# The head of a hybrid backbone: tokens turned, shifted and scaled by pairs of feature chunks while the modulation weights arrive

## Chip, cores and metric

One core of a Trainium2 chip runs the whole kernel. The metric is the device time of one execution in microseconds (us). The engines are TensorE (PE: matmuls, and PEld: its weight loads), VectorE (DVE), ScalarE (ACT), GpSimd (POOL), and SyncE (SP), which issues most of the loads.

## What is computed

Four layers (SSD mixer, attention, pooling mixer, SSD mixer) with one residual stream of 512 tokens (256 of context, 256 latent) and 1024 features. The head works for the first layer alone:

```python
shift, scale, gate = split(silu(c) @ mod_w + mod_b)   # once for the latent tokens' c, once for c_ctx
h = x * (1 + scale) + shift                           # 512 tokens x 1024 features
zxbcdt = h @ w_in                                     # first layer: 1024 -> z, x, B, C, dt
dt = softplus(dt + dt_bias)                           # a chain of small elementwise steps
xbc = silu(depthwise_conv(xbc))                       # five taps
```

## The kernel before

**Exact products.** Every large product is made of three passes. An operand is split into a part rounded for the matmul (`w_hi`, `h_hi`) and the rest (`w_lo`, `h_lo`); `three_pass` (L436 on) multiplies hi by hi, hi by lo and lo by hi into one PSUM bank. ACT makes the hi part (L397 for weights, `act_split`), DVE the lo part (L406, `dve_split`), each behind a load into one of the four slots of `raw`.

**Order.** Each engine runs its own list in the order of the code; counting semaphores tie the lists together. SP issues the loads in the order of `items`: a unit of weights is 1024 columns for 128 partitions, and slot r waits until the unit that lay in it four items earlier is split or summed.

**The head.** The first layer's shift and scale are eight pieces (`HEAD_MODS`) of 256 of the 2048 outputs: pieces 0 to 3 are the shift, 4 to 7 the scale. Each piece comes by two loads of 512 KB to places that are free at that time (`ys`, `xc`, `y`, `xw`, `cb`, `Wa`, `Wb`, `Hs`). For each piece PE makes a sum (`pe_mod_sum`, L466, 16 matmuls with `c_col` as weights), ACT copies the sum out of PSUM (`act_mod_rows`, L486), PE turns it into columns (`pe_mod_turn`, L491), and DVE adds the bias (`dve_mod_col`, L498). The turn of a piece stands behind the sum of the next. The semaphore of a load covers two pieces (`head_full[q // 2]`).

When all eight are in, `dve_ab` (L1688) makes scale and shift columns `ab`; the tokens, turned by PE into features x tokens 128 tokens at a time (`pe_turn`, L1617), are scaled tile by tile, by ACT for tiles 0 and 2 (`act_affine`, L1628, hi part L1634) and by DVE for tiles 1 and 3 (L1667, lo part L1679). `pe_begin` then projects dt and the first x for the first 256 tokens, `ssd_pe_dt` and `ssd_project` with k of 0 and 1 for the other 256. `pe_dt_turn` (L1221) turns the dt rows, and `ssd_dve_start` computes dt from them (L1314 on), with the splits of the first B/C weights (`bc`) and of the second x in between. `taps` (L929) is the convolution; its coefficients `gp` are 24 small copies (L1306, L1308).

Of the kernel before, what the change touches and what calls it, by code (L numbers as in the profile page):

```python
# [3 lines left out]
def backbone(nc, ins, out, depth=4):  # L4
# [4 lines left out]
    F32, F32R = mybir.dt.float32, mybir.dt.float32r  # L9
# [5 lines left out]
    NT = 4  # L15
# [425 lines left out]
    def project(pe, o, key, t, done, t0=0, t1=TOK):  # L441


        for k in range(KT):
# [5 lines left out]
            if done is not None and ((t == 1 and k == KT // 2 - 1) or k == KT - 1):  # L450
                last.then_inc(done, 1)

    def mod_at(L, q):
        return MOD_PIECES * L + q

    def pe_mod_sum(pe, L, q, b):
        for a in range(2):
            if L == 0 and q < HEAD_MODS:
                pe.wait_ge(head_full[q // 2], 64)
                w = head_place(2 * q + a)  # L460
# [195 lines left out]
    def ssd_pe_step(pe, L, i):  # L656
# [4 lines left out]
        if i < GRP:  # L661
            ssd_project(pe, L, i, 0)
# [4 lines left out]
            ssd_project(pe, L, i, 1)  # L667
            if i >= 2:
# [621 lines left out]

    def ssd_dve_start(dve, L):
        s = lay[L]
        j = L // 3
        op, need = dt_steps(dve, s, 0)
        v, e, w, zero = (t256(Wa, k) for k in range(4))
        lnw, r, dtA, dt = (t256(Wb, k) for k in range(4))
        b4 = lambda ap: ap.unsqueeze(1).broadcast_to((128, NT, 2 * HEADS))
        q4 = lambda ap: ap.rearrange("p (c n) -> p c n", c=NT)

        for tap in range(6):  # L1300
# [8 lines left out]
        op("gp", last)  # L1309
        if L:  # L1310
            dve_resid(dve, L - 1, (2, 3))
# [13 lines left out]
        need("zero")  # L1325
        dve_split2(dve, L, "bc", 0)
        dve.wait_ge(s["dt_a"], 4)
# [185 lines left out]
    def pe_tiles_ready(pe, L, n):  # L1513

        s = lay[L - 1] if L else head
        pe.wait_ge(s["hhi_a"], s["base"]["hhi_a"] + n)
        pe.wait_ge(s["hlo_d"], s["base"]["hlo_d"] + n)
# [131 lines left out]

    def act_head_tiles(act):  # L1650

        for n in range(NT):
            if n % 2:
                act.wait_ge(hf_d, n + 1)
            else:
                act_affine(act, head, n, n, n)
            act_h_hi(act, head, n, n)

    def dve_head_tiles(dve):
        for n in (1, 3):  # L1660
            for half in range(2):
                dve.wait_ge(head["turn_p"], 2 * n + half + 1)
                if n == 3:
                    dve.wait_ge(head["hlo_d"], 2)
                for k in range(4):
                    kk = 4 * half + k
                    last = dve.tensor_scalar(hfs[1][:, kk, :], bank[2 * n + half][:, 128 * k:128 * k + 128],  # L1667
                                             ab[:, 0, n // 2, kk:kk + 1], ab[:, 1, n // 2, kk:kk + 1],
                                             ALU.mult, ALU.add)
                last.then_inc(hf_d, 1)  # L1670
            if n == 1:
                dve_split(dve, 0, "x", 0, 1)
            dve_h_lo(dve, head, n - 1, n - 1)
            dve_h_lo(dve, head, n, n)

# [806 lines left out]
    def _(sp):  # L2482
        def load_head(q):
            for a in range(2):
                d = head_place(2 * q + a).rearrange("p (k n) -> p k n", n=256)
                sp.dma_start(d, w_in_view(ins["mod_w"][0], 256 * q, 256, 4 * a, 4 * a + 4)).then_inc(head_full[q // 2], 16)  # L2486
# [55 lines left out]
    def _(act):  # L2542
# [13 lines left out]
        for t in range(NT):  # L2556
# [71 lines left out]
    def _(pe):  # L2628
# [3 lines left out]
        pe.wait_ge(par_done, 2)  # L2632
        for q in range(HEAD_MODS + 1):
            if q < HEAD_MODS:
                pe_mod_sum(pe, 0, q, 6 + q % 2)
            if q:
                if q > 2:
                    pe.wait_ge(mod_done, q - 2)
                pe_mod_turn(pe, 0, q - 1, 4 + (q - 1) % 2)
            if q == 3:  # L2640
                pe.wait_ge(par_loaded, 16 * 10)
                for t in range(1, 5):
                    n = 112 if t == 1 else 128
                    pe.transpose(bank[0][:, 128 * t - 128:128 * t - 128 + n], rows[0:n, t, :],
                                 ident[0:n, 0:n]).then_inc(par_turned, 1)
            if q == 5:
                pe.wait_ge(in_loaded, 64)
                pe_turn(pe, head, 0, 0, (par_done, 6))
                pe_turn(pe, head, 1, 1, (par_done, 6))
        pe_turn(pe, head, 2, 2, (mod_done, HEAD_MODS))  # L2650
        pe_turn(pe, head, 3, 3, (mod_done, HEAD_MODS))
        pe_begin(pe, 0, 0)
        pe_begin(pe, 0, 1)
        for L in range(depth):
            s = lay[L]
            pe_tiles_ready(pe, L, NT)
            if L % 3 == 0:
                ssd_pe_dt(pe, L, SEG, TOK)
                for i in range(GRP + 1):
# [49 lines left out]
```

## Time and profile before

| | us |
|---|---|
| median of 3 runs | 1536.99 (1532.41 to 1537.48) |
| the profiled execution, its own time | 1531.61 |
| its span | 1530.3 |
| PE, DVE, ACT busy | 1455.0, 1132.9, 705.9 |
| last load of head modulation landed | 37.7 |
| first projection begins | 49.6 |
| DVE's dt work begins | 67.1 |
| first convolution tap | 78.4 |

A row of a timeline gives the start, the time from the first start to the last end of its instructions, the engine, the line, what is written and read, and how many instructions are merged. In square brackets stands how long the engine was idle before it, and what ended that. Matmuls overlap, so the pitch between starts tells more than a duration. The span is the time between first and last instruction; the execution's own time also holds what lies around it.

### The profile page before, as it was taken

How to read it: one execution, taken by the hardware profiler on the slowest of the kernel's cores; microseconds unless marked ns; L12 is line 12 of the kernel's file. 1: busy time of each engine (PE TensorE's matmuls, PEld its weight loads, DVE VectorE, ACT ScalarE, POOL GpSimd, SP SyncE). 2: the span in 40 equal slices, each digit the busy share in tenths (PEclk: the TensorE clock that was granted, in tenths of full speed). 3: DMA queues.
4: the chain of work that ended last, by engine and by line, in shares of the span. 5: the costliest groups of instructions: out<-in, count | busy, mean ns of one | idle time of the engine just before them, and what ended most of it. 6: DMA issues, size and time to landing. Idle time of an engine off the chain costs nothing.

```text
span 1530.3 us, 22697 instructions
## 1 busy us (share of the span) xinstructions
PE 1455.0 (95%) x8557; PEld 1205.2 (79%) x8557; DVE 1132.9 (74%) x1694; ACT 705.9 (46%) x1259; POOL 329.0 (21%) x379
## 2 busy tenths in 40 slices
PE   5899999999999999999899999999999999999987
PEld 3787888888877889886678887787888889888865
DVE  0688999999996385867658555646438999999996
ACT  1554554545454253455545322323324565555552
POOL 1042344344451012001000000000001234434340
PEclk9999999999999999999999999999999999999999
DMA  9245535564453413315332436444341444434443
GB/s 325 78 139 168 149 111 167 153 192 133 121 161 130 129 45 87 122 33 174 115 120 88 137 116 195 137 130 165 100 127 29 116 111 129 120 111 115 130 130 122
DMA packets 169421, 197.38 MB, mean 129 GB/s; under 512 B 9696, under 2 KB 151648, under 8 KB 169312
## 3 DMA queue, kind: packets, MB, share of 16 engines
q1 hardware_dynamic: 158480, 163.08, 34.5%
q0 software_dynamic: 9296, 30.19, 7.5%
q10 hardware_dynamic: 1536, 2.67, 0.5%
q8 instruction: 68, 1.11, 0.3%
q14 instruction: 41, 0.34, 0.1%
HBM read 194.59 MB, written 1.31 MB: 128 GB/s over the span
## 4 chain that ended last, share of the span: by engine, by line
PE 45%; DVE 36%; issue 8%; ACT 7%; DMA 2%; SPq 2%; POOL 1%; DVEq 0%; ACTq 0%; POOLq 0%
PE ps L437 12%; PE ps L438 11%; PE ps L439 11%; DVE xc L929 7%; DVE w_lo L406 5%; DVE cum_b L937 4%; ACT w_hi L397 2%; ACT Wb L792 2%; PE ps L466 2%; DVE Wb L956 2%; SPq L2486 1%; DVE Hs L974 1%; PE ps L618 1%; PE ps L1938 1%; PE ps L624 1%
## 5 line engine op out<-in xcount | busy, mean ns | idle before, releaser
L437 PE MATMUL ps<-h_hi,w_hi 128*128 128x512 f32 (+2 forms) x1088 | 412.2, 379 | 9.6 <-issue 4.9
L439 PE MATMUL ps<-h_hi,w_lo 128*128 128x512 f32 (+2 forms) x1088 | 398.6, 366 | 0.0
L438 PE MATMUL ps<-h_lo,w_hi 128*128 128x512 f32 (+2 forms) x1088 | 398.5, 366 | 0.0
L406 DVE TENSOR_TENSOR w_lo<-raw,w_hi 128x1024 fp32r<-128x1024 f32 (+1 forms) x203 | 244.4, 1236 | 112.0 <-ACT w_hi L397 110.3
L397 ACT ACTIVATE w_hi<-raw 128x1024 fp32r<-128x1024 f32 (+1 forms) x203 | 206.5, 1050 | 134.0 <-PE ps L439 114.1
L437 PEld LDWEIGHTS ps<-h_hi,w_hi 128*128 128x128 f32 (+1 forms) x1088 | 205.8, 189 | 54.3 <-issue 19.1
L439 PEld LDWEIGHTS ps<-h_hi,w_lo 128*128 128x128 f32 (+1 forms) x1088 | 205.3, 189 | 33.8
L438 PEld LDWEIGHTS ps<-h_lo,w_hi 128*128 128x128 f32 (+1 forms) x1088 | 205.9, 189 | 30.8
L929 DVE SCALAR_TENSOR_TENSOR xc<-ps,gp,xc 128x508 f32<-128x508 f32 (+1 forms) x224 | 162.7, 727 | 17.9 <-ACT xc L761 12.0
L439 PE MATMUL ps<-w_hi,ylo 128*128 128x512 f32 x376 | 147.1, 391 | 0.0
L1136 POOL DMA_DIRECT2D cum_b<-cum_scratch x96 | 71.8, 754 | 248.0 <-PE ps L618 168.9
L437 PE MATMUL ps<-w_hi,h_hi 128*128 128x512 f32 (+1 forms) x336 | 119.1, 354 | 4.6 <-issue 2.3
L438 PE MATMUL ps<-w_lo,h_hi 128*128 128x512 f32 (+1 forms) x336 | 116.2, 346 | 0.0
L1808 POOL TENSOR_TENSOR small<-small 128x1 f32<-128x1 f32 x14 | 10.4, 741 | 463.5 <-DVE small L1742 463.5
L1155 POOL TENSOR_TENSOR xw<-xT,sg 128x256 f32<-128x256 f32 x96 | 78.9, 852 | 82.0 <-ACT xT L783 82.0
L439 PEld LDWEIGHTS ps<-w_hi,ylo 128*128 128x128 f32 x376 | 71.0, 189 | 15.1
L792 ACT ACTIVATE Wb<-cb,sg 128x128 f32<-128x128 f32 x192 | 58.8, 389 | 44.1 <-DVE cb L947 44.1
L437 PEld LDWEIGHTS ps<-w_hi,h_hi 128*128 128x128 f32 x336 | 64.2, 191 | 14.5 <-issue 3.4
L937 DVE TENSOR_TENSOR cum_b<-cum_b,sg 128x1024 f32<-128x1024 f32 x48 | 72.7, 1515 | 1.2 <-DMA cum_b<-cum_scratch 1.2
L1165 POOL TENSOR_TENSOR Wa<-cb,sg 128x512 f32<-128x512 f32 x48 | 59.1, 1251 | 56.6 <-DVE Wb L956 37.6
L438 PEld LDWEIGHTS ps<-w_lo,h_hi 128*128 128x128 f32 x336 | 64.1, 191 | 7.2
L498 DVE TENSOR_TENSOR mod_col<-ps,par 128x4 f32<-128x4 f32 x48 | 7.6, 157 | 82.5 <-PE ps L491 82.3
(265 smaller groups left out, 2611.4 us busy)
## 6 DMA issues: line engine op xcount, KB each, us to landing
raw<-in_mod_w SPq DMA_DIRECT2D x80, 512.0 KB, 4.6
raw<-in_ssm_w_in SPq DMA_DIRECT2D x64, 512.0 KB, 4.9
cum_b<-cum_scratch POOLq DMA_DIRECT2D x96, 256.0 KB, 5.6
raw<-in_ssm_w_in SPq DMA_DIRECT2D x66, 256.0 KB, 4.6
raw<-in_ssm_w_out SPq DMA_DIRECT2D x32, 512.0 KB, 4.7
raw<-in_pool_w_in SPq DMA_DIRECT2D x32, 512.0 KB, 4.8
raw<-in_attn_w_in SPq DMA_DIRECT2D x20, 512.0 KB, 4.1
raw<-in_pool_w_out SPq DMA_DIRECT2D x16, 512.0 KB, 4.7
```

Of the source, the lines that this page charges most:

```text
L397: act.activation(hi, w_shaped(key, raw[:, r % RS, :], width), ACT.Copy).then_inc(hi_done, 1)
L406: dve.tensor_tensor(lo, w_shaped(key, raw[:, r % RS, :], width), hi.bitcast(F32), ALU.subtract).then_inc(lo_done, 1)
L437: pe.matmul(o, hi_s, hi_m, start=first, stop=False)
L438: pe.matmul(o, hi_s, lo_m, start=False, stop=False)
L439: return pe.matmul(o, lo_s, hi_m, start=False, stop=last)
L466: last = pe.matmul(bank[b][32 * j:32 * j + 32, 0:256], c_col[:, 4 * a + j, :], w[:, 256 * j:256 * j + 256], start=a == 0, stop=a == 1)
L792: last = act.activation(Wb[:, n % 2, h, :], cb[:, 1, c, :], ACT.Copy, scale=sg[:, g, 48 + 4 * c + h:49 + 4 * c + h])
L929: T["tap_d"].inc(dve.scalar_tensor_tensor(ov, iv, gp[:, i, 6 * k + tap:6 * k + tap + 1], ov, ALU.mult, ALU.add))
L937: T["seg_d"].inc(dve.tensor_tensor(e, e, by_head(sg[:, g, 8 * c:8 * c + 8], (128, 8, 128)), ALU.subtract))
L1136: pool.dma_start(cum_b[:, c, d, :, :], src).then_inc(s["cum_loaded"][c], 16)
L1155: last = pool.tensor_tensor(xw[:, k, d, :].rearrange("p (h q) -> p h q", q=PH), xT[:, cs[d], :].rearrange("p (h q) -> p h q", q=PH), sprea ...
L1165: pool.tensor_tensor(Wa[:, n % 2, :, :], cb[:, 0, c, :].unsqueeze(1).broadcast_to((128, HG, 128)), spread(sg[:, g, 32 + 4 * c:36 + 4 * c], ...
```

## The change

Pieces are taken in pairs: piece n of the shift and piece n of the scale (`HEAD_ORDER` is 0, 4, 1, 5, 2, 6, 3, 7). A pair gives shift and scale for two chunks of 128 features, over all 512 tokens. PE turns a chunk (`pe_head_turn`), ACT scales the even chunk and makes both hi parts (`act_head_chunks`), DVE scales the odd one and makes both lo parts (`dve_head_affine`, `dve_head_lo`), and PE adds the chunk's share to dt and the first x, 9 matmuls over 512 columns (`pe_head_project`), before the next pair's sums. The places for the loads and the slots of `raw` are as before; the loads of dt and the first x come behind the first pair, that of the second half of x behind the second pair. The gp copies and the split of the first half of the first `bc` move into the head.

```diff
-        for q in range(HEAD_MODS + 1):
-            if q < HEAD_MODS:
-                pe_mod_sum(pe, 0, q, 6 + q % 2)
-            if q:
-                if q > 2:
-                    pe.wait_ge(mod_done, q - 2)
-                pe_mod_turn(pe, 0, q - 1, 4 + (q - 1) % 2)
...
-        pe_turn(pe, head, 2, 2, (mod_done, HEAD_MODS))
-        pe_turn(pe, head, 3, 3, (mod_done, HEAD_MODS))
-        pe_begin(pe, 0, 0)
-        pe_begin(pe, 0, 1)
+        for n in range(HEAD_MODS + 1):
+            if n < HEAD_MODS:
+                if n >= 2:
+                    pe.wait_ge(mod_done, n - 1)
+                pe_mod_sum(pe, 0, HEAD_ORDER[n], 6 + n % 2)
+            if n:
+                pe_mod_turn(pe, 0, HEAD_ORDER[n - 1], 6 + (n - 1) % 2, 256)
+            if n == 1:
+                pe.wait_ge(in_loaded, 64)
+                for k in range(3):
+                    pe_head_turn(pe, k)
...
+            if n in (3, 5, 7):
+                if n == 3:
+
+                    pe.wait_ge(par_done, 6)
+                for k in (n - 3, n - 2):
+                    pe_head_project(pe, k)
+                for k in {3: (3, 4), 5: (5, 6), 7: (7,)}[n]:
+                    pe_head_turn(pe, k)
+        for k in (KT - 2, KT - 1):
+            pe_head_project(pe, k)
```

ACT's and DVE's lists, and the new functions that they call:

```diff
+        for n, q in enumerate(HEAD_ORDER):
+            act_mod_rows(act, 0, q, 6 + n % 2)
+            if n == 1:
+                act_split(act, 0, "dt", 0, 0, width=KT * 64)
+                act_split(act, 0, "x", 0, 0)
...
+            if n % 2:
+                act_head_chunks(act, n // 2)
+            if n == 3:
+                act_split(act, 0, "x", 0, 1)
+        act_split(act, 0, "bc", 0, 0)
...
+        for n, q in enumerate(HEAD_ORDER):
+            dve_mod_col(dve, 0, q, 6 + n % 2, 256)
+            if n % 2:
+                dve_head_ab(dve, n // 2)
+                dve_head_affine(dve, n // 2)
+                if n == 1:
+                    dve_split(dve, 0, "dt", 0, 0, width=KT * 64)
+                    dve_split(dve, 0, "x", 0, 0)
+                dve_head_lo(dve, n // 2)
+            if n == 3:
+                dve_split(dve, 0, "x", 0, 1)
+            if n == 5:
+                dve.wait_ge(par_done, 6)
+                ssd_dve_taps_par(dve, 0)
+        dve_split(dve, 0, "bc", 0, 0)
...
+    def act_head_chunks(act, n):
+
+        k = 2 * n
+        act.wait_ge(head["ab_d"], n + 1)
+        act.wait_ge(head["turn_p"], k + 1)
+        if n >= 2:
+            act.wait_ge(head["hlo_d"], k - 3)
+        for st in range(2):
+            c = slice(SEG * st, SEG * st + SEG)
+            last = act.activation(head_hf(k)[:, c], head_bank(k)[:, c], ACT.Identity, scale=ab[:, 0, st, k:k + 1],
+                                  bias=mod_col[:, 0, k, st:st + 1])
+        last.then_inc(head["hf_a"], 1)
+        act.wait_ge(head["hf_a"], n + 1)
+        act.activation(h_hi[:, k, :], head_hf(k), ACT.Copy).then_inc(head["hhi_a"], 1)
+        act.wait_ge(hf_d, n + 1)
+        act.activation(h_hi[:, k + 1, :], head_hf(k + 1), ACT.Copy).then_inc(head["hhi_a"], 1)
...
+    def pe_head_project(pe, k):
+
+        s = lay[0]
+        pe.wait_ge(head["hhi_a"], k + 1)
+        pe.wait_ge(head["hlo_d"], k + 1)
```

And SP's, where a load's place in the list is its turn:

```diff
-        for q in range(HEAD_MODS - 2):
-            load_head(q)
+        for n in range(2):
+            load_head(n)
         for r, (kind, n, key) in enumerate(items):
-            if r == 2:
-                for q in range(HEAD_MODS - 2, HEAD_MODS):
-                    load_head(q)
+
+            if r in (2, 3):
+                for n in range(2, 4) if r == 2 else range(4, HEAD_MODS):
+                    load_head(n)
```

**How the order moves.** On PE before, from the fifth sum to the first projection (`xc`, `y`, `xw`, `cb` and so on are places of the loaded pieces, `pick` turns a sum, `resid` are the tokens):

```order
L466 MATMUL ps<-xc,c_col 32x256 x8
L491 MATMUL ps<-pick,mod_rows 128x2 x2
L466 MATMUL ps<-y,c_col 32x256 x4
L466 MATMUL ps<-xw,c_col 32x256 x4
L491 MATMUL ps<-pick,mod_rows 128x2 x2
L1617 MATMUL ps<-ident,resid 128x128 x16
...
L491 MATMUL ps<-pick,mod_rows 128x2 x4
L1617 MATMUL ps<-ident,resid 128x128 x16
L437 MATMUL ps<-h_hi,w_hi 64x256
```

On PE in the changed kernel, the same pieces, from the last matmul of chunk 1 on:

```order
L1698 MATMUL ps<-h_hi,w_lo 128x512
L1679 MATMUL ps<-ident,resid 128x128 x8
L470 MATMUL ps<-xc,c_col 32x256 x8
L495 MATMUL ps<-pick,mod_rows 128x2 x2
L470 MATMUL ps<-y,c_col 32x256 x4
L470 MATMUL ps<-xw,c_col 32x256 x4
L495 MATMUL ps<-pick,mod_rows 128x2 x2
L437 MATMUL ps<-h_hi,w_hi 64x512
```

The first L495 row completes a pair; the second belongs to the next pair, and it stands between that completion and the projection of chunks 2 and 3.

On ACT in the changed kernel, the second pair, from the copy of its second sum (the copies of sums are L490, the chunks L1713 to L1719, the split L397):

```order
L490 ACTIVATE mod_rows<-ps 128x256
L1713 ACTIVATE hf<-ps,mod_col,ab 128x256 x2
L1717 ACTIVATE h_hi<-hf 128x512
L1719 ACTIVATE h_hi<-hf 128x512
L397 ACTIVATE w_hi<-raw 128x1024
L490 ACTIVATE mod_rows<-ps 128x256 x2
```

The copy of the next pair's first sum, for which PE's second L495 row waits, stands behind the chunks and the split. Before, no copy of a sum had a token operation ahead of it: the copies of sums were done when the first L1628 came.

## Rows read from the trace of the kernel before

**Rows 1.** The page's chain that ended last, shares by engine

```profile
PE 45%; DVE 36%; issue 8%; ACT 7%; DMA 2%; SPq 2%; POOL 1%; DVEq 0%; ACTq 0%; POOLq 0%
```

**Rows 2.** The chain in order of time, 0 to 130 us: start, us, what

```profile
28.00 9.74 DMA Hs<-in_mod_w
...
43.13 2.91 ACT hf L1628 x8
...
66.66 0.41 PE ps L1221 x4
67.09 0.44 DVE Wa L1314
...
76.04 2.35 DVE w_lo L406 x2
78.39 0.67 DVE xc L929
```

**Rows 3.** Timeline of PE, 0 to 125 us

```profile
21.65 1.94 PE L466 MATMUL ps<-ys,c_col 128*32 128x256 f32 x16 [4.67 <-DMA ys<-in_mod_w]
...
26.32 1.01 PE L491 MATMUL ps<-pick,mod_rows 128*128 128x2 f32 x4
...
33.75 3.65 PE L1617 MATMUL ps<-ident,resid 128*128 128x128 f32 x16
...
38.59 0.60 PE L466 MATMUL ps<-Wa,c_col 128*32 128x256 f32 x8
...
41.90 0.58 PE L491 MATMUL ps<-pick,mod_rows 128*128 128x2 f32 x4 [0.62 <-DVE mod_col L498]
42.73 1.97 PE L1617 MATMUL ps<-ident,resid 128*128 128x128 f32 x16 [0.26 <-DVE mod_col L498]
49.62 0.45 PE L437 MATMUL ps<-h_hi,w_hi 128*64 128x256 f32 x1 [4.92 <-issue]
...
54.55 0.41 PE L439 MATMUL ps<-h_hi,w_lo 128*64 128x256 f32 x1
...
70.73 0.50 PE L437 MATMUL ps<-h_hi,w_hi 128*128 128x512 f32 x1 [0.60 <-DVE w_lo L406]
...
76.08 0.39 PE L439 MATMUL ps<-h_hi,w_lo 128*128 128x512 f32 x1
```

**Rows 4.** Busy time by stretch: PE, PEld, DVE, ACT, POOL, granted clock, DMA, GB/s

```profile
core 0: us, PE busy (x) PEld busy (x) DVE busy (x) ACT busy (x) POOL busy (x), PEclk, DMA share, GB/s
...
28.00:32.00 4.00, 4.00 (x34) 2.06 (x36) 0.16 (x1) 1.15 (x5) 1.78 (x3) 1.00 1.10 334
...
50.00:52.00 2.00, 2.00 (x12) 2.00 (x11) 2.00 (x8) 1.97 (x5) 0.00 (x0) 0.50 0.09 29
```

**Rows 5.** Timeline of ACT, 0 to 125 us

```profile
24.63 0.38 ACT L486 ACTIVATE mod_rows<-ps 128x256 f32<-128x256 f32 x1 [7.16 <-PE ps L491]
...
34.26 1.56 ACT L397 ACTIVATE w_hi<-raw 128x512 fp32r<-128x512 f32 x2
...
41.65 1.05 ACT L397 ACTIVATE w_hi<-raw 128x1024 fp32r<-128x1024 f32 x1
...
63.83 0.59 ACT L1253 ACTIVATE y<-ps 64x512 f32<-64x512 f32 x1 [10.41 <-PE ps L439]
...
71.96 1.43 ACT L761 ACTIVATE xc<-ps,gp 128x512 f32<-128x512 f32 x2
```

**Rows 6.** Timeline of DVE, 0 to 125 us

```profile
42.51 0.16 DVE L498 TENSOR_TENSOR mod_col<-ps,par 128x4 f32<-128x4 f32 x1 [0.76 <-PE ps L491]
...
43.13 2.64 DVE L1667 TENSOR_SCALAR hf<-ps,ab 128x128 f32<-128x128 f32 x8
45.70 1.21 DVE L406 TENSOR_TENSOR w_lo<-raw,w_hi 128x1024 fp32r<-128x1024 f32 x1
...
56.45 0.17 DVE L1308 COPY gp<-par 128x8 f32<-128x8 f32 x1
...
115.59 0.68 DVE L970 COPY Hs<-ps 128x512 f32<-128x512 f32 x1
```

More of the change, by code:

```diff
@@ L451, in project @@
                 last.then_inc(done, 1)
+    HEAD_ORDER = [q for n in range(HEAD_MODS // 2) for q in (n, HEAD_MODS // 2 + n)]
     def mod_at(L, q):
-        return MOD_PIECES * L + q
+        return MOD_PIECES * L + (HEAD_ORDER.index(q) if L == 0 and q < HEAD_MODS else q)
     def pe_mod_sum(pe, L, q, b):
@@ L1294, in ssd_dve_start @@
         op, need = dt_steps(dve, s, 0)
[L1295 to L1298, printed above, removed]
         for tap in range(6):
@@ L1309, in ssd_dve_start @@
         op("gp", last)
+    def ssd_dve_start(dve, L):
+        s = lay[L]
+        if L:
+            ssd_dve_taps_par(dve, L)
+        op, need = dt_steps(dve, s, 1)
+        v, e, w, zero = (t256(Wa, k) for k in range(4))
+        lnw, r, dtA, dt = (t256(Wb, k) for k in range(4))
+        b4 = lambda ap: ap.unsqueeze(1).broadcast_to((128, NT, 2 * HEADS))
+        q4 = lambda ap: ap.rearrange("p (c n) -> p c n", c=NT)
         if L:
@@ L1325, in ssd_dve_start @@
         need("zero")
-        dve_split2(dve, L, "bc", 0)
+        for a in range(2) if L else (1,):
+            dve_split(dve, L, "bc", 0, a)
         dve.wait_ge(s["dt_a"], 4)
@@ L1648, in dve_affine_half, with head_bank @@
         last.then_inc(s["hf_a"], 1)
[L1650 to L1674, printed above, removed]
+    def head_bank(k):
+        return bank[(2, 4, 5)[k % 3]]
@@ new lines, in head_hf, with pe_head_turn @@
+    def head_hf(k):
+        return hfs[k // 2 % 2][:, :, :].rearrange("p k n -> p (k n)")[:, 512 * (k % 2):512 * (k % 2) + 512]
+    def pe_head_turn(pe, k):
+        if k >= 3:
+            pe.wait_ge(*((hf_d, (k - 3) // 2 + 1) if k % 2 == 0 else (head["hf_a"], (k - 3) // 2 + 1)))
+        for tt in range(NT):
+            last = pe.transpose(head_bank(k)[:, 128 * tt:128 * tt + 128], resid[:, tt, 128 * k:128 * k + 128],
+                                ident[:, :])
+        last.then_inc(head["turn_p"], 1)
@@ new lines, in pe_head_project @@
+    def pe_head_project(pe, k):
+        s = lay[0]
+        pe.wait_ge(head["hhi_a"], k + 1)
+        pe.wait_ge(head["hlo_d"], k + 1)
+        hi, lo = pe_unit(pe, 0, "dt", 0, 0)
+        c = slice(64 * k, 64 * k + 64)
+        last = three_pass(pe, bank[3][0:64, :], hi[:, c], lo[:, c], h_hi[:, k, :], h_lo[:, k, :], k == 0, k == KT - 1)
+        if k == KT - 1:
+            last.then_inc(s["dt_p"], 1)
+        hi, lo = pe_unit(pe, 0, "x", 0, k // 4)
+        for t in range(2):
+            c = slice(256 * (k % 4) + 128 * t, 256 * (k % 4) + 128 * t + 128)
+            pe.matmul(bank[t], hi[:, c], h_hi[:, k, :], start=k == 0, stop=False)
+            mid = pe.matmul(bank[t], hi[:, c], h_lo[:, k, :], start=False, stop=False)
+            last = pe.matmul(bank[t], lo[:, c], h_hi[:, k, :], start=False, stop=k == KT - 1)
+            if k == KT - 1:
+                if t == 1:
+                    mid.then_inc(s["x_p"], 1)
+                last.then_inc(s["x_p"], 1)
@@ new lines, in dve_head_ab, with dve_head_affine @@
+    def dve_head_ab(dve, n):
+        k = 2 * n
+        dve.wait_ge(mod_done, k + 2)
+        dve.tensor_scalar(ab[:, 0, :, k:k + 2].rearrange("p s k -> p k s"), mod_col[:, 0, KT + k:KT + k + 2, :],
+                          1.0, None, ALU.add).then_inc(head["ab_d"], 1)
+    def dve_head_affine(dve, n):
+        k = 2 * n + 1
+        dve.wait_ge(head["ab_d"], n + 1)
+        dve.wait_ge(head["turn_p"], k + 1)
+        if n >= 2:
+            dve.wait_ge(head["hhi_a"], k - 3)
+        for st in range(2):
+            c = slice(SEG * st, SEG * st + SEG)
+            last = dve.tensor_scalar(head_hf(k)[:, c], head_bank(k)[:, c], ab[:, 0, st, k:k + 1],
+                                     mod_col[:, 0, k, st:st + 1], ALU.mult, ALU.add)
+        last.then_inc(hf_d, 1)
@@ L1676, in dve_h_lo, with dve_head_lo @@
+    def dve_head_lo(dve, n):
+        dve.wait_ge(hf_d, n + 1)
+        for k in (2 * n, 2 * n + 1):
+            dve.wait_ge(head["hhi_a"], k + 1)
+            dve.tensor_tensor(h_lo[:, k, :], head_hf(k), h_hi[:, k, :].bitcast(F32),
+                              ALU.subtract).then_inc(head["hlo_d"], 1)
     def dve_h_lo(dve, s, n, tt):
```

68 lines of the change are left out of this document (27 added, 41 removed).

## The prediction

> **What bounds the kernel now.** I read the page's chain first: PE and DVE hold 45% and 36% of it, DMA 2% [rows 1]. The kernel is no load-bound kernel as a whole, but its first 50 us are another stage. So the chain in order of time comes next, for the head alone [rows 2]: it stands on the last of the eight pieces of modulation weights until 37.7 us (28.00 + 9.74), then on turns, shift and scale, and the scaling of the tokens (8 ACT operations from 43.13), and only at 49.62 does the first projection begin [rows 3]. The four dt transposes at 66.66 release DVE's dt work at 67.09; that runs to the weight splits at 76.04 and to the first convolution tap at 78.39 [rows 2]. From there DVE is named again and again, so the number that decides is not when PE finishes x, but **when DVE can start its dt work: 67.1 us today** (call it V).
>
> The head's projections are slow at first: PE had waited 4.92 us, and the 24 dt matmuls of 256 columns from 49.62 to 54.55 have a pitch of (54.55 - 49.62)/23 = 0.214 us, with the granted clock at 0.50 in 50 to 52 [rows 3, 4], i.e. 1.2 GHz. At the full clock a 512-column matmul has a pitch of (76.08 - 70.73)/23 = 0.233, less one late start; I take 0.228. Before 38 us the page's clock says 1.00, but sixteen equal transposes took 3.65 us at 33.75 and 1.97 us at 42.73 [rows 3]: I read the early stretch as slow too, rising about 38.4, between the 3.65 us of transposes and the sum at 38.59.
>
> **The change, part by part.** The total of the loads stays; one x piece (0.52 MB) moves ahead of the last four pieces of modulation. At 334 GB/s [rows 4] the last load comes 1.6 us later, 39.3.
>
> A round is now, in PE's order: sum of a piece, turn of the one before, sum, turn, project two chunks (18 matmuls of 512 columns), transpose further chunks. The turn that completes a pair stands ahead of the projection of the same pair, and the next pair's sums stand behind it. So a pair's whole chain through ACT and DVE lies open on PE. I price it from a turn's start T:
> - turn to DVE's column 0.61 (41.90 to 42.51), the column 0.16 and a scale like it, 0.4 with their starts [rows 3, 6].
> - two ACT affines of 256 columns out of PSUM: 128 columns cost 2.91/8 = 0.36, 512 cost 1.43/2 = 0.72, so 0.48 each, 1.0 together [rows 2, 5]. DVE's pair beside it: 0.33 at 128, 0.68 at 512 [rows 6], so 0.45 each, hidden.
> - two ACT copies of 512: 1.56 less the 1.05 of 1024 columns gives 0.5 to 0.6 each [rows 5]; DVE's h_lo of 512: half of 1.21, 0.65 [rows 6].
>
> The even chunk can be projected at T + 3.4, the odd one at T + 4.0. But PE first waits for the next piece's turn, and that waits for ACT's copy of the sum (0.38), which stands behind ACT's chunks: T + 4.0 in the third pair, and in the second, where the second x piece's split (1.05) stands there too, T + 5.0 [rows 5].
>
> *First pair.* Its second turn stands behind the sum of the third piece, so it waits for the second pair of loads: before, that sum began at 21.65, released by the load [rows 3]; dt and x (0.79 MB) now go ahead of it, + 2.35 = 24.0. Sum 1.9 (21.65), turn at 25.9, 1.0 at the slow clock (26.32): DVE's column at 27.0. ACT's chunks are done at 29.65, its copy of the next sum at 30.0, PE's turn at 31.0. DVE has two splits (1.8) ahead of its h_lo: ready at 30.9. **The first projection starts at 31.0.** Its price: 18 x 0.228 = 4.1 at full clock, 18 x 0.427 = 7.7 at half clock (twice the 0.214 of 256 columns). The rate rose 4.8 us after the dense work from 33.75 began, and from 49.62 it had not risen by 54.55 [rows 3]. I take 5.4 us: 12.6 slow matmuls and 5.4 fast ones, 6.6 us; ends 37.6.
>
> *Later rounds*, full clock: eight transposes 1.0 (half of 1.97), a sum 0.95 (8 matmuls 0.60 with the tail of the last, so under twice that, 38.59). Second pair's T = 37.6 + 1.95 = 39.55; projection T + 5.0 to T + 9.1; transposes and sum 1.95: third pair's T = 50.6. Projection T + 4.0 to T + 8.1, four transposes 0.5: last T = 59.2. Last projection T + 3.4 to T + 7.5 = 66.7. All loads are in at 39.3, so most of this lies after them: **only the first pair is really projected during the loads**. The dt rows are complete at 65.4, ACT's copy of them (0.6) hides, PE's transposes start at 66.7, and V = 67.2 against 67.1.
>
> *What V does not show.* 144 matmuls of 256 columns become 72 of 512: the same columns. The 24 small copies to gp move into DVE's wait for the last turn, 59.2 + 0.6 by the schedule, and cost nothing; bare they would be at most 24 x 0.17 = 4.1 us [rows 6]. The first bc split leaves the dt chain: such a pair costs 2.35 at 76.04, so 1.2 us on DVE [rows 2]; but ACT reads the dt rows at 65.4 rather than 63.8 [rows 5], so its table load, exponent and bc copy end 0.5 later, and its Exp and Ln with them. I keep 0.6 of the 1.2. PE can project bc's first half at once and then waits for the second, no longer the bound. Sum at the first tap: + 0.1 - 0.6 = **- 0.5 us**. Against the profiled execution's 1531.6 that is 1531.1; that execution lies 5.4 us below the median of the runs shown (1536.99), so the same change on the median gives 1536.5.
>
> Unknown costs, both ends. The slow stretch of the first pair: 4.1 (none slow) to 7.7 (all slow), - 2.5 to + 1.1. The three open chains, 5.0 + 4.0 + 3.4: a quarter less or more is 3.1 either way, since nothing in the trace shows 256-column affines. The clock in the later pairs: below.
>
> The notes bear on this too. Profile first: behind the sixteen transposes of 33.75 the next sums ran at the fast rate, and the transposes of 42.73 themselves took half the time [rows 3]. The Trainium skill (TensorE: Matmul & The Clock Gate, "Part 4: PE-mode transpose") says that the full clock does not engage for transposes. By that rule the transposes between my rounds would not help to hold the clock; here the trace does not agree, and the sum stays as it is.
>
> **Rivals.**
> *The clock falls between the rounds (slower).* Place: PE's wait between the second sum and the blocking turn. In the trace it fell after PE had gone idle at 44.7, and stood at half in 50 to 52 [rows 3, 4]; the complete waits of my schedule are 2.5, 1.5 and 2.9 us, shorter, but little work stands around them, only sums and turns. A pair that runs slow costs 18 x 0.2 = 3.6 us. One such pair gives + 3.1, not measurable; from two on it decides: + 6.7, 1543.7; all three with their sums and transposes about + 12, 1549. For it: the early sums up to 32 us ran slow for long. Against it: from 38.6 to 44.7 sums and turns kept the rate up. 0.16.
> *The rounds are shorter than I price (faster).* No slow stretch in the first pair and a third off the open chains: - 2.5 - 4.1 - 0.5 = - 7, 1530. For it: ACT's and DVE's chain after the loads today, on four times as many instructions, runs without gaps [rows 2]. 0.16.
> *The loads bound every round.* Then only the last pair lies behind 39.3: two sums, two turns 3.3, chain 2.8, projection 4.1, V = 50, - 17 us, 1520. It needs all three earlier projections done by 39; by the sum only one is. 0.03.
> *The change does nothing for what follows:* x is ready sooner, and the dt chain or the POOL loads behind it swallow the 0.5. 1537.0. 0.10.
> The forecast itself: 0.55.
>
> **How the numbers follow.** About 0.3% (4.6 us) is what a measurement of this kernel can tell from no change. Same: 0.55 + 0.10 = 0.65. Faster: 0.16 + 0.03 = 0.19. Slower: 0.16. The likeliest case's own range is - 4 to + 4 around 1536.5. To leave out no more than 2 in 10, the range goes from the second rival's 1530 (with a little, 1529) to 1542, which leaves out most of the slow-clock case and the load-bound one.
>
> **What would show it.** In the profile of the changed kernel: the first projection at 31, three waits of PE of 2 to 3 us each ahead of a turn of mod_rows or of a projection, named by ACT's mod_rows or h_lo; the last x matmul near 66.7; DVE's dt work at 67.2; a tap at 77.9. Each pair's 18 matmuls: 4.1 us at full rate, 7.7 at half. The prediction is wrong if V lies under 63 or over 71: then the pitch of the pairs tells the clock, and the start of each against its turn tells the chain.

## The result: 0.6% slower, half of it in the head

The changed kernel took 1544.5 us (median of 4), the kernel before 1536.1 beside it: a ratio of 1.0058, 95% interval 1.0039 to 1.0077. A second set of runs gave 1542.6 against 1532.8, 1.0060 (1.0045 to 1.0075): **+ 9 us, between 7 and 11.5** by the second, narrower interval. The profiled execution took 1542.85 us, its span 1541.6. The forecast was 1536.5 and no change that can be measured.

The chain in order of time stands on ACT's scaling of a chunk once per pair. The last three of the four, some 12 us apart, are shown here; [rows 2] had this link once:

```profile
40.40 1.03 ACT hf L1713 x2
...
53.10 1.03 ACT hf L1713 x2
...
64.81 1.03 ACT hf L1713 x2
...
82.62 0.67 DVE xc L936
```

The first tap stands at 82.6 instead of 78.4 in this view (82.5 and 78.3 in DVE's timeline, which the table below uses). The timeline of PE has each round's start, to be read beside [rows 3]:

```profile
31.55 0.66 PE L437 MATMUL ps<-h_hi,w_hi 128*64 128x512 f32 x1
...
37.39 1.03 PE L1679 MATMUL ps<-ident,resid 128*128 128x128 f32 x8
...
39.35 0.61 PE L495 MATMUL ps<-pick,mod_rows 128*128 128x2 f32 x4
...
43.87 0.61 PE L495 MATMUL ps<-pick,mod_rows 128*128 128x2 f32 x4 [2.58 <-ACT mod_rows L490]
44.34 0.43 PE L437 MATMUL ps<-h_hi,w_hi 128*64 128x512 f32 x1
...
50.08 1.04 PE L1679 MATMUL ps<-ident,resid 128*128 128x128 f32 x8
...
52.05 0.61 PE L495 MATMUL ps<-pick,mod_rows 128*128 128x2 f32 x4
...
56.48 0.67 PE L437 MATMUL ps<-h_hi,w_hi 128*64 128x512 f32 x1
...
57.37 0.63 PE L439 MATMUL ps<-h_hi,w_lo 128*64 128x512 f32 x1
57.80 0.63 PE L1696 MATMUL ps<-h_hi,w_hi 128*128 128x512 f32 x1
...
63.43 0.60 PE L1679 MATMUL ps<-ident,resid 128*128 128x128 f32 x4
63.87 0.51 PE L495 MATMUL ps<-pick,mod_rows 128*128 128x2 f32 x4
67.39 0.41 PE L437 MATMUL ps<-h_hi,w_hi 128*64 128x512 f32 x1 [3.02 <-ACT h_hi L1719]
```

Turn to projection is 5.0 us in the second pair (39.35 to 44.34), 4.4 in the third (52.05 to 56.48), 3.5 in the last; 5.0, 4.0 and 3.4 were worked out ahead. What differs is the length of the pairs: 44.34 to 50.08 and 56.48 to 63.43 are 5.7 and 6.95 us for 18 matmuls that take 4.1 at full rate. In the third pair two matmuls of 512 columns are 0.43 us apart (57.37 and 57.80), not 0.228. The granted clock says why (busy times by stretch; columns as in [rows 4], the clock is the last but two):

```profile
40.00:42.00 2.00, 1.07 (x16) 0.42 (x16) 1.33 (x4) 1.56 (x4) 0.00 (x0) 1.00 1.13 310
42.00:44.00 2.00, 0.13 (x1) 0.13 (x2) 1.64 (x3) 1.82 (x4) 0.00 (x0) 1.00 0.27 85
44.00:46.00 2.00, 2.00 (x10) 1.54 (x11) 0.95 (x2) 0.39 (x1) 0.00 (x0) 0.86 0.01 3
46.00:48.00 2.00, 2.00 (x6) 1.34 (x5) 0.00 (x0) 0.00 (x0) 0.00 (x0) 0.50 0.85 245
...
60.00:62.00 2.00, 2.00 (x6) 1.26 (x5) 0.00 (x0) 0.00 (x0) 0.00 (x0) 0.50 0.00 0
```

PE waits (0.13 us of work in 42 to 44), and about 1 us after it has begun to project, the clock goes to 1.2 GHz in the middle of the work. V, DVE's first dt operation, comes out at 72.14; the forecast was 67.2, the kernel before had 67.1:

```profile
72.14 0.42 DVE L1329 TENSOR_TENSOR Wa<-ps,dtb_b 128x256 f32<-128x256 f32 x1 [2.85 <-PE ps L1228]
```

The head thus explains 4.2 of the 11.3 us between the two spans. The rest arises far behind it, in good part at three places at which the changed kernel's trace has a lower clock. First the kernel before, then the changed kernel 4 to 8 us later, at the same three places in the work:

```profile
485.00:492.00 7.00, 6.27 (x32) 5.04 (x31) 2.38 (x2) 4.32 (x6) 0.00 (x0) 1.00 0.06 9
751.00:762.00 11.00, 11.00 (x95) 8.26 (x93) 6.73 (x17) 7.23 (x20) 0.00 (x0) 0.84 0.52 168
1054.00:1059.00 5.00, 5.00 (x32) 3.82 (x25) 0.00 (x0) 0.38 (x1) 0.00 (x0) 1.00 0.63 217
```

```profile
489.00:496.00 7.00, 6.27 (x20) 4.77 (x19) 0.69 (x1) 2.47 (x4) 0.00 (x0) 0.51 0.00 1
758.00:769.00 11.00, 10.59 (x74) 7.82 (x76) 5.92 (x18) 7.72 (x22) 0.00 (x0) 0.69 0.38 114
1062.00:1067.00 5.00, 5.00 (x28) 3.34 (x29) 0.16 (x1) 0.42 (x2) 0.00 (x0) 0.66 0.66 231
```

Length times missing clock gives what these stretches can cost at most: 7 x 0.49 = 3.4, 11 x (0.84 - 0.69) = 1.7, 5 x 0.34 = 1.7. What they did cost is read from one and the same DVE operation in both traces. The changed kernel is late by 4.1 us at 469 us of the kernel before, 6.8 at 510, 8.0 at 745, 8.7 at 775 and at 1045, 10.4 at 1080 (the table of these stands with the second traces below). So the three places hold 2.8, 0.7 and 1.7 us, 5.2 of the missing 7.1. Another 1.1 us came between 690 and 745 us, where both traces grant the full clock; its cause was not looked into.

### The profile page after: what moved, and what is told of

Same layout as the page of the kernel before. It is cut to its first block, busy times and chain, and to the rows that moved or that the text cites. A ratio compares the mean times of both kernels' runs of the same rounds, so it can differ in the third digit from the quotient of the medians.

```text
span 1541.6 us, 22556 instructions
## 1 busy us (share of the span) xinstructions
PE 1461.6 (95%) x8485; PEld 1205.2 (78%) x8485; DVE 1132.5 (73%) x1690; ACT 704.1 (46%) x1255; POOL 329.1 (21%) x379
## 4 chain that ended last, share of the span: by engine, by line
PE 46%; DVE 35%; issue 7%; ACT 7%; DMA 2%; POOL 1%; SPq 1%; DVEq 0%; ACTq 0%; POOLq 0%
PE ps L437 12%; PE ps L438 11%; PE ps L439 11%; DVE xc L936 7%; DVE w_lo L406 5%; DVE cum_b L944 4%; ACT w_hi L397 2%; ACT Wb L799 2%; PE ps L470 2%; DVE Wb L963 2%; DVE Hs L981 1%; PE ps L622 1%; PE ps L2009 1%; PE ps L1993 1%; PE ps L628 1%
## 5 line engine op out<-in xcount | busy, mean ns | idle before, releaser
L437 PE MATMUL ps<-h_hi,w_hi 128*128 128x512 f32 (+2 forms) x1048 | 401.9, 383 | 8.2 <-DVE w_lo L406 5.1
L439 PE MATMUL ps<-h_hi,w_lo 128*128 128x512 f32 (+2 forms) x1048 | 388.4, 371 | 0.0
L438 PE MATMUL ps<-h_lo,w_hi 128*128 128x512 f32 (+2 forms) x1048 | 388.3, 371 | 0.0
L397 ACT ACTIVATE w_hi<-raw 128x1024 fp32r<-128x1024 f32 (+1 forms) x203 | 206.6, 1050 | 137.6 <-PE ps L439 116.5
L437 PEld LDWEIGHTS ps<-h_hi,w_hi 128*128 128x128 f32 (+1 forms) x1048 | 198.3, 189 | 53.5 <-issue 14.4
L439 PEld LDWEIGHTS ps<-h_hi,w_lo 128*128 128x128 f32 (+1 forms) x1048 | 197.9, 189 | 35.0 <-issue 0.8
L438 PEld LDWEIGHTS ps<-h_lo,w_hi 128*128 128x128 f32 (+1 forms) x1048 | 198.3, 189 | 31.4 <-issue 0.4
L1879 POOL TENSOR_TENSOR small<-small 128x1 f32<-128x1 f32 x14 | 10.4, 740 | 469.3 <-DVE small L1813 469.3
L439 PEld LDWEIGHTS ps<-w_hi,ylo 128*128 128x128 f32 x376 | 71.5, 190 | 15.3
L1172 POOL TENSOR_TENSOR Wa<-cb,sg 128x512 f32<-128x512 f32 x48 | 59.1, 1251 | 56.7 <-DVE Wb L963 37.7
```

Of the source, the lines that this page charges most:

```text
L397: act.activation(hi, w_shaped(key, raw[:, r % RS, :], width), ACT.Copy).then_inc(hi_done, 1)
L437: pe.matmul(o, hi_s, hi_m, start=first, stop=False)
L438: pe.matmul(o, hi_s, lo_m, start=False, stop=False)
L439: return pe.matmul(o, lo_s, hi_m, start=False, stop=last)
L1172: pool.tensor_tensor(Wa[:, n % 2, :, :], cb[:, 0, c, :].unsqueeze(1).broadcast_to((128, HG, 128)), spread(sg[:, g, 32 + 4 * c:36 + 4 * c], ...
```

## Experiments

Each ratio is against the kernel before, run on the same chip beside it. The kernel before had medians of 1532.8 to 1536.1 in the four sets, so kernels are compared by their ratios. V and the first tap are from one trace each, and in two traces of the kernel before V differs by 1.6. All times in us.

| kernel | V | first tap | median | ratio (95% interval) |
|---|---|---|---|---|
| before, first and second trace | 67.1, 68.7 | 78.3, 79.9 | 1532.8 to 1536.1 | |
| changed, first and second trace | 72.1, 72.8 | 82.5, 83.2 | 1544.5, 1542.6 | 1.0058 (1.0039 to 1.0077), 1.0060 (1.0045 to 1.0075) |
| changed, waits filled | 67.1 | 77.5 | 1535.4 | 1.0008 (0.9996 to 1.0020) |
| changed, turns late | 69.2 | 79.5 | 1538.8 | 1.0029 (1.0017 to 1.0040) |
| one pair later | 59.8 | 70.1 | 1529.4 | 0.9968 (0.9957 to 0.9979) |
| one pair later, warmed | 61.1 | 71.5 | 1530.3 | 0.9973 (0.9962 to 0.9983) |
| one pair later, dt first | 59.7 | 70.1 | 1529.9 | 0.9967 (0.9954 to 0.9980) |
| one pair later, 32 extra matmuls | 69.7 | 79.8 | 1535.9 | 1.0004 (0.9990 to 1.0018) |
| before, 9 extra matmuls | 68.7 | 79.9 | 1537.2 | 1.0015 (1.0002 to 1.0027) |
| before, 18 extra matmuls | 71.4 | 82.6 | 1539.9 | 1.0035 (1.0021 to 1.0049) |
| changed, 9 extra matmuls | 76.2 | 86.3 | 1544.8 | 1.0057 (1.0039 to 1.0076) |
| before, bc split early | 66.3 | 76.4 | 1535.4 | 1.0005 (0.9993 to 1.0018) |

### The waits filled: is it the clock?

```diff
+            pe_fill(pe, {5: 9, 7: 6}.get(n, 0))
             if n:
                 pe_mod_turn(pe, 0, HEAD_ORDER[n - 1], 6 + (n - 1) % 2, 256)
...
+        pe_fill(pe, 12)
         for k in (KT - 2, KT - 1):
             pe_head_project(pe, k)
...
+    def pe_fill(pe, count):
+        for c in range(count):
+            pe.matmul(bank[0], w_hi[:, 1, 0:128], h_hi[:, 0, :], start=False, stop=False)
```

> The changed kernel, with PE's three open waits filled by extra 512-column matmuls that nothing waits for (9 ahead of the turn of piece 5's predecessor, 6 two pieces later, 12 ahead of the last two chunks); they add the first chunk's term to x's first bank again, so x is not the reference's. Theory clock: V (DVE's first dt operation, 72.1 in the changed kernel, 67.1 before) is late because pairs 2 and 3 ran 3.3 and 6.8 us at half rate; filled, both pairs take 4.1 us and V comes to 67.5 to 68.5, the time falls by some 4 us against the changed kernel, to about 1540. Theory chain: the open waits for ACT and DVE are the loss and the clock is incidental; V stays within 1 us of 72, the time at 1544.

The extra matmuls add to x's first bank, so that bank holds more than x here; the kernel is there for the measurement alone.

```profile
43.55 0.61 PE L495 MATMUL ps<-pick,mod_rows 128*128 128x2 f32 x4 [0.29 <-ACT mod_rows L490]
44.02 0.42 PE L437 MATMUL ps<-h_hi,w_hi 128*64 128x512 f32 x1
...
48.21 1.04 PE L1679 MATMUL ps<-ident,resid 128*128 128x128 f32 x8
...
54.22 0.42 PE L437 MATMUL ps<-h_hi,w_hi 128*64 128x512 f32 x1
...
58.40 0.60 PE L1679 MATMUL ps<-ident,resid 128*128 128x128 f32 x4
```

In PE's timeline the turn that waited 2.58 us now waits 0.29, both pairs take 4.2 us, and V is 67.12. With 27 matmuls more, the kernel is by the two ratios 0.5%, some 8 us, faster than the changed one and no longer told apart from the kernel before. The clock theory holds for the head; the rival (V within 1 us of 72) is out. The time fell by more than the expected 4: V fell by 5.0, the rest came back behind the head. So filling PE's waits in the head takes back the whole loss, also the part that arises behind it.

### The blocking turn moved behind the projection

```diff
-            if n:
+            if n and n not in (5, 7):
                 pe_mod_turn(pe, 0, HEAD_ORDER[n - 1], 6 + (n - 1) % 2, 256)
...
                 for k in (n - 3, n - 2):
                     pe_head_project(pe, k)
+                if n > 3:
+                    pe_mod_turn(pe, 0, HEAD_ORDER[n - 1], 6 + (n - 1) % 2, 256)
```

> The changed kernel, with the first turn of pairs 3 and 4 placed behind the projection of the chunks before it instead of ahead of it. Theory queue (the copy of the next sum stands behind ACT's chunk work and PE waits for it): pair 2 starts 3.5 us after its turn instead of 5.0, pair 3 3.5 instead of 4.4, V comes 2.5 us earlier by itself, and the shorter waits may also keep the clock up, up to 4 more: V 66 to 69.6, time 1538 to 1542. Theory chain (PE has to wait for h_lo all the same): V moves by less than 1 us, time 1544.

```profile
43.85 0.41 PE L437 MATMUL ps<-h_hi,w_hi 128*64 128x512 f32 x1 [1.69 <-ACT h_hi L1719]
...
54.01 0.42 PE L437 MATMUL ps<-h_hi,w_hi 128*64 128x512 f32 x1 [1.69 <-ACT h_hi L1719]
...
62.83 0.42 PE L437 MATMUL ps<-h_hi,w_hi 128*64 128x512 f32 x1 [3.02 <-ACT h_hi L1719]
```

Turn to projection is 3.6 us in every pair (the turns at 40.22, 50.38 and 59.20), the waits 1.7, 1.7 and 3.0, and only behind the last one did the clock fall. V 69.2 and 1538.8 lie where the queue theory put them. The two chains are together 2.2 us shorter (1.4 and 0.8); some 0.7 of that goes to the two turns that now stand behind the projections (48.02 to 48.38, 58.17 to 58.53). The rest of the gain at V is time at half rate that is no longer there.

### Each pair projected one pair later

The instructions are the same; PE makes the next pair's sums and turns first. The core of the edit:

```diff
-            if n in (3, 5, 7):
-                if n == 3:
-
+            for k in {1: (0, 1, 2), 3: (3, 4), 5: (5, 6), 7: (7,)}.get(n, ()):
+                pe_head_turn(pe, k)
+            if n in (4, 6, 8):
+                if n == 4:
                     pe.wait_ge(par_done, 6)
-                for k in (n - 3, n - 2):
+                for k in (n - 4, n - 3):
                     pe_head_project(pe, k)
```

> The changed kernel, with each pair projected one pair later: PE makes the next pair's two sums and turns first, and the projection (4.1 us) covers the chain of ACT and DVE (3.4 to 4.0 us). The same instructions on all engines. Theory order (PE's order, not the loads or the number of operations, makes the head slow): projections start at 33 to 34, run densely at full rate from 38 on, the last load at 41 is followed by two sums and turns and two pairs: V 56 to 58, 10 us before the kernel before; time 1524 to 1529. Theory load or engine bound (ACT and DVE need the time anyway): V 66 or more, time 1536 or more.

```profile
35.28 0.61 PE L495 MATMUL ps<-pick,mod_rows 128*128 128x2 f32 x4
35.75 0.42 PE L437 MATMUL ps<-h_hi,w_hi 128*64 128x512 f32 x1
...
43.49 0.61 PE L495 MATMUL ps<-pick,mod_rows 128*128 128x2 f32 x4
43.96 0.42 PE L437 MATMUL ps<-h_hi,w_hi 128*64 128x512 f32 x1
...
50.38 0.61 PE L495 MATMUL ps<-pick,mod_rows 128*128 128x2 f32 x4
50.84 0.42 PE L437 MATMUL ps<-h_hi,w_hi 128*64 128x512 f32 x1
```

No projection waits any more: each begins 0.5 us after a turn, in these rows without a bracket of idle time. V is 59.75, 7 to 9 us ahead of the kernel before, and the time is **0.32% (0.21 to 0.43) below the kernel before**, some 4.9 us, and by the two ratios 0.9% below the changed kernel. V and time both fall short of what was expected (56 to 58, 1524 to 1529): from 24.8 to 59 us PE has no wait over 0.2 us, and until about 35 it works at half rate. Not all of V's lead reaches the end: in its trace the same DVE operations are 7.1 us ahead of the first trace of the kernel before at 469 us, 5.1 at 775, 3.4 at 1080. This is the version to keep.

### The early stretch warmed, and the dt rows first

```diff
+                for c in range(12):
+                    pe.transpose(bank[2][:, 128 * (c % 4):128 * (c % 4) + 128], ident[:, :], ident[:, :])
                 pe.wait_ge(in_loaded, 64)
+                for c in range(12):
+                    pe.transpose(bank[2][:, 128 * (c % 4):128 * (c % 4) + 128], resid[:, c % 4, 0:128], ident[:, :])
```

> The version that projects one pair later, with 24 transposes more while PE waits for loads at 16 to 25 us (12 of the identity, 12 of tokens, all overwritten by the right ones). There PE is busy without a gap from 24.8 to 59 us, half rate until about 35. Theory clock (the early stretch is bound by PE at half rate, and transposes can raise the rate): sums and turns from 25 us on take half the time, the first projection starts at 33 to 34 (32 is the second load of the pair), all later pairs shift with it until the last load, V 57 to 58 against 59.75, time 1 to 3 us less. The page's rule that transposes don't bring the full clock: nothing changes, or V is up to 1 us later by the added work.

```profile
16.56 2.80 PE L2723 MATMUL ps<-ident 128*128 128x128 f32 x12
19.32 2.56 PE L2726 MATMUL ps<-ident,resid 128*128 128x128 f32 x12
21.72 1.47 PE L1679 MATMUL ps<-ident,resid 128*128 128x128 f32 x12
...
33.08 1.94 PE L470 MATMUL ps<-xc,c_col 128*32 128x256 f32 x16 [2.48 <-DMA xw<-in_mod_w]
```

Twelve transposes fall from 2.80 to 1.47 us, with nothing but transposes in the 5 us ahead of that (sums and a turn stand ahead of these). The trace of the next version, without the extra transposes, has a purer case: PE is idle for 3.11 us, its 12 transposes from 19.54 on take 2.82 us (granted clock 0.50 in 20 to 22, 0.89 in 22 to 24), and the sum behind them takes 1.07 us, not the 1.93 that the same sum takes in the version without the warming.

```profile
19.54 2.82 PE L1679 MATMUL ps<-ident,resid 128*128 128x128 f32 x12 [3.11 <-DMA resid<-in_x]
24.70 1.07 PE L470 MATMUL ps<-ys,c_col 128*32 128x256 f32 x16 [2.34 <-DMA ys<-in_mod_w]
```

So the clock rose with only transposes at work. The Trainium skill (TensorE: Matmul & The Clock Gate, "Part 4: PE-mode transpose") says that the full clock does not engage for transposes; if it means transposes like these, of float32 by the identity, the two traces do not agree. The warmed version did not pay: the sums finish early, PE waits 2.48 us for the fifth piece's load, the sum behind that is slow again (1.94 us), and V is 61.1, where 57 to 58 was expected. The time stays that of the version without.

The other edit splits `pe_head_project` into its dt and x parts and ends with them in this order:

```diff
-        for k in (KT - 2, KT - 1):
-            pe_head_project(pe, k)
+        for k, parts in ((KT - 2, "d"), (KT - 1, "d"), (KT - 2, "x")):
+            pe_head_project(pe, k, parts)
+        pe_dt_turn(pe, 0)
+        pe_head_project(pe, KT - 1, "x")
```

> The version that projects one pair later, with the dt rows of chunks 6 and 7 projected before the x of chunks 6 and 7, and the dt transposes put ahead of the last x chunk. V is bound by the dt rows, not by x. The rows are complete after chunk 7's lo part, some 4.6 us after the last turn (50.4 in the version it starts from, V 59.75 there): dt complete 55.5 to 56.3, V 57.5 to 58.3, tap 1.5 to 2 us earlier, time 1 to 2 less. Rival: PE has to wait for chunk 7 (ready 4.0 after the turn) because less work stands ahead of it, and nothing is won: V 59 or more.

From the last turn to V it is 8.0 us (51.72 to 59.69) instead of 9.4 (50.38 to 59.75), so the edit gives its 1.4 us. V itself is 59.7 where 57.5 to 58.3 was expected: in that trace the first pair was slow until 39.5, which took the gain back. In the medians the two versions are not told apart.

### How much is the head, how much what lies behind it

Extra matmuls into a free bank, 0.23 us each, ahead of the turn of the dt rows, in three kernels:

```diff
             if i == 0:
+                for c in range(18 if L == 0 else 0):
+                    pe.matmul(bank[6], w_hi[:, 1, 0:128], h_hi[:, 0, :], start=True, stop=True)
                 pe_dt_turn(pe, L)
```

18 of them in the kernel before:

> The kernel before, with 18 extra matmuls of 512 columns into a free bank ahead of the turn of the dt rows: the head is 4.1 us longer, V 71.2, and nothing else is touched. The changed kernel was 8.4 us slower with a V only 5.0 and a first tap only 4.2 later. Theory shift plus chance: a later head costs its own length, the rest is slow stretches of the clock at other places that fall differently in each run: 1540 to 1541 here. Theory amplification: a head of this length is followed by more slow stretches behind it: 1543 to 1545, like the changed kernel.

9 in the kernel before:

> The kernel before with 9 extra matmuls instead of 18 ahead of the turn of the dt rows: the head 2.05 us longer. 18 cost 5.8 us by the medians and 4.3 at V. Theory shift plus chance: 2 to 3 us. Theory that where the head ends decides which of PE's later waits lose the clock: not in proportion, anything from 0 to 6 us, and the stretches at half rate behind 80 us stand at other places than with 18 (there 489 to 496 and 759 to 766).

9 in the changed kernel:

> The changed kernel with 9 extra matmuls ahead of the turn of the dt rows: V 2 us later, 74 to 75. A fixed cost behind the head: 2 us above the changed kernel, about 1545 against a kernel before at 1533. Alignment of the later waits: 0 to 6 us above it, or even below.

32 in the version one pair later:

> The version that projects one pair later, with 32 extra matmuls ahead of the turn of the dt rows, 7.3 us, so that V is that of the kernel before (67.0). If V and the tap are all that the head gives to the rest, the time is the kernel before's less the 0.8 of the shorter dt chain: -3 to +2 us of it. If the chunked head leaves a cost of its own behind it (other places of the waits, other loads), 3 us or more above it.

The pure delays of 4.3 us (measured at V) and 2.05 (by count) cost 5.4 (3.2 to 7.5) and 2.3 (0.3 to 4.1): no proof of an amplification. In the changed kernel 9 more matmuls put V 4.1 us later, twice their own length, since the second and third pair had some 3 us more at half rate; even so the time did not rise (1.0057 after 1.0058 and 1.0060). And the version one pair later, brought to V 69.7 (67.0 was aimed at) and a tap at 79.8, level with the second trace of the kernel before, took the time of the kernel before (1.0004, - 1.5 to + 2.8 us). So in that version chunks, loads and places leave no cost behind the head that this can tell. What moves are the stretches at half rate. The place at 489 us, in turn in the kernel with 18 extra matmuls, and in the changed kernel with 9:

```profile
489.00:496.00 7.00, 6.17 (x18) 4.92 (x19) 0.16 (x1) 2.78 (x5) 0.00 (x0) 0.52 0.02 8
```

```profile
491.00:498.00 7.00, 5.10 (x30) 4.01 (x31) 1.08 (x3) 3.10 (x5) 1.05 (x1) 1.00 0.30 109
```

### The same two kernels again

> The changed kernel once more, with a second trace and more timed runs beside the kernel before. Two traces gave a first tap 4.2 us later but a span 11.3 us longer; 7.3 us of that is time at half rate (53.9 us against 39.3 in the whole trace), at the same places in which the kernel with 18 extra matmuls had it (489 to 496, 759 to 766). Theory chance: where PE waits a few us, a run may or may not lose the clock, so a second trace shows other stretches behind 80 us, and the median lies 5 to 7 us over the kernel before. Theory of a fixed cost behind the head: the same stretches again, the median 8 to 10 over.

> The kernel before once more, for a second trace. Theory chance: V within 1 us of 67.1 or up to 3 off where the slow stretch of the first projections falls otherwise, and other stretches at half rate behind 80 us than in the first trace, more of them than its 39.3 us, since that trace was one of the fastest runs (1531.6 against a median of 1534 to 1537). Theory fixed: the same stretches and 1531 to 1532.

(The 53.9 and 39.3 us of the expectations count time behind the span too; inside it they are 52.3 and 37.7, with the same difference.) The second trace of the changed kernel has 1.00 where the first had 0.51:

```profile
489.00:496.00 7.00, 6.02 (x30) 4.86 (x30) 1.80 (x2) 4.31 (x7) 0.04 (x1) 1.00 0.02 8
758.00:769.00 11.00, 10.16 (x63) 7.44 (x65) 6.29 (x17) 7.78 (x21) 0.00 (x0) 0.69 0.34 104
1062.00:1067.00 5.00, 5.00 (x28) 3.67 (x29) 0.16 (x1) 0.80 (x2) 0.00 (x0) 0.66 0.78 267
```

So the place at 489 is a matter of the run. The other two are slow in both traces of the changed kernel. But they are slow in the second trace of the kernel before as well, so they do not set the two kernels apart. That trace has V at 68.7 and took 1535.7, and it also shows what the first did not record, the early stretch at half rate:

```profile
20.00:30.00 10.00, 8.39 (x60) 4.26 (x60) 0.33 (x2) 1.54 (x6) 0.67 (x1) 0.50 1.12 332
...
751.00:762.00 11.00, 10.12 (x68) 7.38 (x70) 6.33 (x17) 7.72 (x21) 0.00 (x0) 0.69 0.35 108
1055.00:1060.00 5.00, 4.94 (x28) 3.30 (x29) 0.16 (x1) 0.88 (x3) 0.00 (x0) 0.66 0.71 239
```

How much later than in the first trace of the kernel before one and the same DVE operation starts, in us:

| start in the first trace of before | before, second | changed, first | changed, second |
|---|---|---|---|
| 99.8 | 1.6 | 4.2 | 4.9 |
| 469.3 | 1.6 | 4.1 | 4.6 |
| 509.9 | 1.6 | 6.8 | 4.6 |
| 689.9 | 1.6 | 6.8 | 4.6 |
| 710.8 | 1.6 | 7.5 | 5.6 |
| 744.7 | 1.4 | 8.0 | 8.4 |
| 775.0 | 2.1 | 8.7 | 9.0 |
| 1044.8 | 2.2 | 8.7 | 9.1 |
| 1079.8 | 3.7 | 10.4 | 10.7 |
| 1500.3 | 3.8 | 10.5 | 11.5 |

The step of 1.6 us between 1045 and 1080 is in all three columns. Against the second trace of the kernel before, both changed traces fall behind by another 4 to 5 us between 469 and 1500 us, but mostly at different places: the first at 489, the second between 711 and 745, where the granted clock is 0.83 (730 to 740; 1.00 in the other three traces). So the two theories of the expectation come out mixed: the slow stretches changed place, as chance would have it, but the median lies 9.8 us over the kernel before, as a fixed cost would.

### The early bc split alone

```diff
         act_head_tiles(act)
+        act_split(act, 0, "bc", 0, 0)
...
-        dve_split2(dve, L, "bc", 0)
+        for a in range(2) if L else (1,):
+            dve_split(dve, L, "bc", 0, a)
```

> One part of the change alone: the kernel before with the first half of the first B/C weights split at the end of the head instead of inside the dt chain. Theory of the prediction (ACT and DVE stand idle there from 53 and 56 us to 64 and 67): the split costs nothing there and takes 1.2 us of DVE and 1.0 of ACT out of the chain, V stays at 67.1, the tap comes 0.6 to 1.1 earlier; the time 0.5 to 1 less, not measurable by itself. Rival (the chain is bound by ACT's table loads and its Exp and Ln): the tap moves by less than 0.3.

```profile
66.33 0.42 DVE L1315 TENSOR_TENSOR Wa<-ps,dtb_b 128x256 f32<-128x256 f32 x1 [8.79 <-PE ps L1221]
...
76.41 3.09 DVE L929 SCALAR_TENSOR_TENSOR xc<-ps,gp,xc 128x508 f32<-128x508 f32 x4
```

From V to the first tap it is 10.1 us instead of the 11.2 of both traces of the kernel before. So the split leaves the chain as forecast, with 1.1 of its 1.2 us, too few for the medians to show.

## Why the prediction was wrong

**What bounds the head: right in the main.** Filled to V 67.1, the changed kernel is level with the kernel before, and so is the later version when delayed to V 69.7. But time does not follow V one for one: 7 to 9 us at V were worth 4.9, and 4.1 us at V in the changed kernel nothing.

**The schedule up to 44 us: right within 0.6.** First projection 31.55 (forecast 31.0), first pair's end 37.4 (37.6; here two errors cancel, the start 0.55 late and the pair 5.8 us instead of 6.6), second pair's turn 39.35 (39.55), its projection 44.34 (44.55). The open chains of 5.0, 4.0 and 3.4 us measured 5.0, 4.4 and 3.5. That nearly all the projection lies behind the loads was right too.

**The step that failed: "Later rounds, full clock".** The term of 18 x 0.228 = 4.1 us for each later pair measured 5.7, 6.95 and 4.2, and the turn ahead of the third ran slow as well (0.4). That is 4.9 us, all of the error in V (72.14 against 67.2); with the waits filled, V came to 67.12. I had the mechanism as a rival with a chance of 0.16 and compared the waits of 2.5, 1.5 and 2.9 us with the one long idle time in the trace. What the trace had not shown was a short wait between sums and turns, and such waits were followed by the fall: in 40 to 44 us PE's busy time was 1.2 of 4. They are not always: the longest wait, 3.02 us ahead of the last pair, left the clock at 1.00 in the first trace (64 to 70 us), while behind the same wait the second trace has 0.50 in 68 to 70. I also priced the rival by its cost in the head alone; that its 1543.7 for two slow pairs lies near the measured 1544.5 is luck, since half of the loss arose behind the head.

**The second error: that the median moves by what V moves.** The head's part is 4.2 us at the tap (3.7 by the means of two traces each). The measured + 7 to + 11.5 holds some 3 to 8 us more. That they are no fixed cost of the chunked head is shown within 3 us by the version one pair later when delayed, and filling PE's waits in the head takes them away. Between the first traces 5.2 us of them stand at three places with a lower clock. But two of the three are slow in the second trace of the kernel before too, and the third is not slow in the second trace of the changed kernel, which lost time between 711 and 745 us instead. Whether the waits in the head make such losses more frequent, or whether the runs merely fell so, stays open.

**Right in the small.** The dt chain: V to tap 10.4 against 11.2, 0.8 us less where 0.6 was kept. The gp copies cost nothing. The load-bound rival is out: V never came near 50, even in the version without open waits.

## What to carry to other kernels

Cutting a stage into rounds turns one chain between engines into several, and each lies open unless the engine has other work to do meanwhile: put the next round's start ahead of this round's bulk, as the version one pair later does with the same instructions (12 us at V and 0.9% of the time between the two orders). Price PE's work behind even a short wait at both levels of the clock, above all where only sparse matmuls stand around the wait. And look at what stands in an engine's queue between the instruction that starts a chain and the one that uses it: here a turn that belonged to the next pair.

## What the hardware showed that I had not expected

- The clock fell after waits of PE of 2.58 and 1.64 us with thin work around them. The first time it fell in the middle of dense matmuls, about 1 us after they had begun again (0.86 granted in 44 to 46, 0.50 in 46 to 48). After a wait of 3.02 us it fell in one trace of the same kernel and not in the other.
- The clock rose behind 12 transposes that had 3.11 us of idle time ahead of them: 2.82 us for the transposes, 1.07 for the sum behind them.
- Useless matmuls paid: 27 of them in PE's waits took 8 us off the changed kernel, which made it level with the kernel before.
- The profile's clock can say 1.00 for a stretch that runs at half rate, as long as no change of it has been recorded: the first trace of the kernel before says 1.00 for 28 to 32 us, the second 0.50 for 20 to 30.
